# Two of the matmuls' operand buffers begin eight bytes later in on-chip memory

## The reference

```python
def first_block(x, ...):                       # two layers
    for layer in range(2):
        h = rmsnorm(x, attn_norm[layer])
        x = x + (even_mixer(h, ...) if layer == 0 else mla_mixer(h, ...))
        h = rmsnorm(x, ffn_norm[layer])
        x = x + (silu(h @ w_gate[layer]) * (h @ w_up[layer])) @ w_down[layer]   # 1024 -> 2816 -> 1024
    return rmsnorm(x, final_norm)

def second_block(x, ...):                      # one layer
    proj = rms_norm(x, g) @ w_in               # 1024 -> 3328
    y = rwkv7_mix(proj[:, :1792], ...)         # a recurrence over the tokens, in chunks
    o = diff_attention(...)
    h = x + rms_norm(concat(y, o) @ w_out, g)
    u = causal_dwconv(rms_norm(h, g) @ w_up)   # 1024 -> 5632
    return h + rms_norm((gelu(u[:, :2816]) * u[:, 2816:]) @ w_down, g)
```

## Time and profile before

| | us |
|---|---|
| median of 3 runs | 1925.72 |
| lowest, highest | 1923.92, 1926.21 |
| span of the profiled execution | 1924.0 |
| PE busy in it | 1890.1 |
| PEld busy | 1527.6 |
| DVE, ACT, POOL busy | 999.1, 740.1, 179.1 |

### The profile page before, as it was taken

How to read it: one execution, slowest core, us unless ns; L and a number is a source line. 1 busy time by engine, 2 the same in 40 slices (tenths; PEclk the granted TensorE clock), 3 DMA queues, 4 the chain that set the end, 5 groups by cost and what they waited for, 6 DMA issues and landing times.

```text
span 1924.0 us, 26779 instructions
## 1 busy us (share of the span) xinstructions
PE 1890.1 (98%) x10729; PEld 1527.6 (79%) x10729; DVE 999.1 (52%) x1418; ACT 740.1 (38%) x1111; POOL 179.1 (9%) x215
## 2 busy tenths in 40 slices
PE   9999999999999999999999999999999999999998
PEld 7875788888888777788888888777878778888887
DVE  5456453434325686553343434749563566656523
ACT  4247432222224575542222323554342454333322
POOL 1001210000001100010000000303551100000001
PEclk9999999999999999999999999999999999999999
DMA  6310133232322202123223232321120223232321
GB/s 201 105 44 1 50 99 98 87 109 87 105 92 80 72 23 66 45 91 105 91 87 109 88 109 87 100 88 44 24 67 25 88 77 109 87 108 89 107 90 66
DMA packets 137795, 158.74 MB, mean 83 GB/s; under 512 B 15976, under 2 KB 125552, under 8 KB 137712
## 3 DMA queue, kind: packets, MB, share of 16 engines
q1 hardware_dynamic: 136272, 155.01, 25.2%
q0 software_dynamic: 1440, 2.58, 0.5%
HBM read 153.89 MB, written 3.68 MB: 82 GB/s over the span
## 4 chain that ended last, share of the span: by engine, by line
PE 90%; DVE 6%; ACT 2%; issue 1%; DMA 0%; SPq 0%; POOL 0%; ACTq 0%; DVEq 0%
PE bank L2893 35%; PE bank L2926 16%; PE bank L2425 13%; PE bank L2450 3%; PE bank L2980 2%; PE bank L2569 2%; PE bank L2944 2%; PE bank L2839 1%; PE bank L2872 1%; PE bank L2597 1%; PE bank L2688 1%; PE bank L2584 1%; PE bank L2511 1%; PE bank L2541 1%; DVE XL L1589 1%
## 5 line engine op out<-in xcount | busy, mean ns | idle before, releaser
L2893 PE MATMUL bank<-XH,w_hi 128*128 128x512 f32 x992 | 386.8, 390 | 0.7 <-DVE arena L1889 0.7
L2893 PE MATMUL bank<-XL,w_hi 128*128 128x512 f32 x992 | 386.0, 389 | 0.0
L2893 PE MATMUL bank<-XH,w_lo 128*128 128x512 f32 x992 | 385.9, 389 | 0.0
L2893 PEld LDWEIGHTS bank<-XH,w_hi 128*128 128x128 f32 x992 | 186.2, 188 | 39.9 <-DVE arena L1889 0.9
L2893 PEld LDWEIGHTS bank<-XL,w_hi 128*128 128x128 f32 x992 | 186.2, 188 | 39.1 <-issue 0.5
L2893 PEld LDWEIGHTS bank<-XH,w_lo 128*128 128x128 f32 x992 | 186.2, 188 | 38.8
L2425 PE MATMUL bank<-XH,w_hi 128*128 128x512 f32 x448 | 178.7, 399 | 2.5 <-DVE w_lo L1582 2.4
L2425 PE MATMUL bank<-XH,w_lo 128*128 128x512 f32 x448 | 175.3, 391 | 0.0
L2425 PE MATMUL bank<-XL,w_hi 128*128 128x512 f32 x448 | 175.1, 391 | 0.0
L1582 DVE TENSOR_TENSOR w_lo<-w_raw,w_hi 128x2048 fp32r<-128x2048 f32 (+5 forms) x67 | 116.4, 1757 | 93.9 <-ACT w_hi L1036 93.5
L1936 DVE TENSOR_TENSOR w_lo<-w_raw,w_hi 128x2048 fp32r<-128x2048 f32 x24 | 55.0, 2292 | 174.2 <-ACT w_hi L1347 174.2
(11 more groups left out here) (459 smaller groups left out, 3336.1 us busy)
## 6 DMA issues: line engine op xcount, KB each, us to landing
w_raw<-in_ffn_w_gate SPq DMA_DIRECT2D x22, 1024.0 KB, 5.3
w_raw<-in_ffn_w_up SPq DMA_DIRECT2D x22, 1024.0 KB, 5.3
w_raw<-in_ffn_w_down SPq DMA_DIRECT2D x22, 1024.0 KB, 4.9
w_raw<-in_w_up SPq DMA_DIRECT2D x22, 1024.0 KB, 5.1
w_raw<-in_w_in SPq DMA_DIRECT2D x13, 1024.0 KB, 5.3
w_raw<-in_w_down SPq DMA_DIRECT2D x11, 1024.0 KB, 5.0
w_raw<-in_even_w_in SPq DMA_DIRECT2D x8, 1024.0 KB, 5.3
w_raw<-in_even_w_out SPq DMA_DIRECT2D x4, 1024.0 KB, 5.3
```

What stands on the lines that cost most here:

```text
L2893: m = pe.matmul(bank[b][:, :], w[:, k, P * c:P * (c + 1)], x[:, k, :], start=(k == 0 and j == 0), stop=(k == KT - 1 and j == 2))
```

## The change

The function that places a buffer takes an alignment; a buffer of two words is put ahead of `XH`, and `XH`, `XL` and the float32 view under them are placed at multiples of 8 bytes instead of 32. No instruction is added, removed or moved on any engine.

```diff
-        def sb(name, shape, dt=F32):
-            return ctx.enter_context(nc.sbuf_tensor(name, shape, dt))
+        def sb(name, shape, dt=F32, align=32):
+            return ctx.enter_context(nc.sbuf_tensor(name, shape, dt, align_bytes=align))
...
         X = sb("X", [P, KT, SEQ])
-        with nc.sbuf_tensor("under_split", [P, 2 * KT * SEQ], F32) as under_split:
+        sb("two_words", [P, 2])
+        with nc.sbuf_tensor("under_split", [P, 2 * KT * SEQ], F32, align_bytes=8) as under_split:
             pass
-        XH = sb("XH", [P, KT, SEQ], F32R)
-        XL = sb("XL", [P, KT, SEQ], F32R)
+        XH = sb("XH", [P, KT, SEQ], F32R, align=8)
+        XL = sb("XL", [P, KT, SEQ], F32R, align=8)
         w_raw = sb("w_raw", [P, 2, UW])
```

## The result

| | before | after |
|---|---|---|
| median, us | 1925.47 (4 runs) | 1963.79 (4 runs) |
| lowest to highest | 1923.92 to 1926.21 | 1961.72 to 1965.68 |
| span of the profiled execution | 1924.0 | 1962.7 |
| PE busy | 1890.1 | 1929.3 |

The kernel is slower by 38.3 us, a ratio of 1.02 with a 95% interval of 1.0188 to 1.0212. The prediction was 1968.7, range 1922 to 1985. TensorE is at the high level of its clock in both profiles (granted clock 0.995 and 0.997 of full speed).

What follows compares the result with a forecast made beforehand. PE was taken to bound the kernel, busy 1890.1 of 1924.0 us. Matmuls of 512 columns (40.4 us) and 256 columns (2.5 us) made +43 us, other parts 0: span 1967, median 1968.7 us, range 1922 to 1985.

Steps and rivals of the forecast that it cites:

- the 6120: Matmuls of 512 columns counted in L2893, L2425, L2926, L2980, L2839 and L2439; at 6.6 ns each, 40.4 us more.
- 24 is nearer to 32 than to 0: Reason for charging the new 24-byte operand distance the whole 6.6 ns a matmul seen at 32 bytes.
- Eight bytes as such: Operands beginning two words past a multiple of 16 bytes: taken as 0; no row showed a moving one.
- the second sign of being wrong: Forecast wrong altogether if the eight bytes matter in their own right on the moving side; no size given.
- A: Rival: nothing happens, under_arena's products are slow from its place far up in memory; 1925.7 us, chance 0.22.
- B: Rival: in L2893, L2425 and L2926 shifted reads lose half of the 12.9 ns on top; 1886 us, chance 0.12.
- C: Rival: 512 moving columns touch one more 16-byte line, 1.7 ns on each matmul; 1936 us, chance 0.08.
- D: Rival: the moving operand's start needs more reads, worse than 32 bytes, 13.2 ns each; +86 us, 2012 us, chance 0.08.

Runs made afterwards that it cites:

- the stretches: Not the model: matmuls alone, mostly 144 in L2893's three passes, operands' places varied; 227.0 ns a matmul at distance 0, 230.1 to 234.3 at thirty of 31 distances from 4 to 124 bytes.

## Why the prediction came out right

The direction, the mechanism (the rhythm of the matmul stream, through the operands' places) and the price of a matmul were right; some things in it were not.

**The sum.** L2893 is exact: 2976 x 6.6 ns = 19.6 us were forecast, and its three loops took 235.21 - 228.53 us twice and 224.31 - 217.94 once, 19.7 us. L2425 got 6.8 ns a matmul in a long piece (39.22 us for 168; 38.08 before) and about 6.4 on average of the pieces that can be compared, with 1344 of them 8.6 us, against 8.9 forecast. L2926 was over-sized: its pieces with activations moving went from 104.09 to 107.29 us, twice, and its 480 matmuls with weights moving lost 4.4 ns instead of 6.6, 2.1 us; 9.5 us were forecast and 8.5 came. L2450 had the wrong sign: 384 x 6.6 ns = +2.5 us were forecast, and it gained 2.0 ns each, -0.8 us. These two terms are 4.3 of the 4.9 us by which the forecast was too high. The step that failed in L2450 is the carrying of a price from 512 moving columns to 256; the stretches with 256 columns show that there most unequal distances are the faster ones. There is also a gap in the count: 240 matmuls of 512 columns on `XH`, `XL`, `w_hi` and `w_lo` in smaller groups (48 each in L2450, L2750, L3298 and L2872, 24 each in L2459 with L2462 and in L2489) are not among the 6120. At 6.6 ns they would have put 1.6 us more on the forecast; under 1 us came, 4 to 6 ns each in the pieces of L2750, L2459, L2489 and L3298 that can be compared.

**Why 24 bytes cost as much as 32.** The forecast took "24 is nearer to 32 than to 0". The choice was right and the reason wrong: the price doesn't grow with the distance. In the stretches 4 bytes already cost 5.3 ns, more than the 4.1 of 24 bytes with the moving operand in its old place. That the changed kernel's own pair costs the price of 32 bytes was luck: the prediction had no row for it.

**Eight bytes as such.** The prediction left the moving operand's eight bytes open and took them at nothing beside the distance. With both operands eight bytes off the model takes 232.1 ns at equal remainders, so they do count by themselves: the second sign of being wrong, that the eight bytes matter in their own right, came true beside the forecast. They add nothing at 32 bytes' distance, since the change and the 32 bytes alone both take 233.3 ns.

**The rest.** ACT, DVE and the transfers were put at 0, and nothing of them is seen in the time; L2944 was said to stay, and stayed (233.3 and 233.1 ns). A loses twice: the distance alone slows the model, and 224 bytes more heal `first_down`. The Trainium skill, "TensorE: Matmul & The Clock Gate", Part 2, gives TensorE two independent read ports, one for each operand. What the prediction drew from this for A, that the distance can't matter, doesn't hold here: it costs 37 us in the model with the weights 32 bytes further on. Whether the two ports are independent no run here shows. B (faster) came true only in L2450, for 0.8 us. C forecast 1.7 ns a matmul; with both operands eight bytes off it is 5.4, and with `XH` and `XL` at their old places and only the weights moved it is 6.6. The Trainium skill, "SBUF — State Buffer", specifications, says that each step to a new line of 16 bytes has a price; no run here shows such a price apart from the rhythm. D's 13.2 ns were not seen; the worst of all stretches, both operands 4 bytes off, is 10.8 above the fast one.

**What stays open** is why. The prediction laid it to the weight load that reads while the matmul streams. A load that is 81 ns shorter made a matmul 4.7 ns longer in line and 3.4 ns shorter at 32 bytes, where some 10 and 14 ns less were expected, and at 384 moving columns the distance makes no difference. So the length of the load isn't what is paid. An interplay of the two reads in time isn't excluded by that, nor shown. What is shown is a stream of float32r matmuls whose distance from start to start depends on the places of all its operands. The exception at 120 bytes is open too.

## What to carry to other kernels

When a matmul-bound kernel runs in float32r with 512 moving columns, look at the time from one matmul's start to the next: give all moving and stationary buffers the same remainder mod 256 and start them at multiples of 32 bytes, and look for the odd buffer that isn't (here `under_arena`, 1923.08 against 1925.35 us). A buffer added or resized between the activations and the weights cost 2% here without touching an instruction, while 32 bytes ahead of both cost nothing, so print the addresses when a time moves for no reason. Before carrying a price to another width of the moving operand, find a row with that width.

## What the hardware showed that wasn't expected

- One buffer is enough to lose the fast rhythm: `XL`, `w_hi` or `w_lo` alone off by 32 bytes costs 4.0, 4.9 or 6.2 ns a matmul in the mean of the whole stream.
- In the distances tried it comes back at 256 bytes, not at 128: at a distance of 128 bytes a matmul takes 232.4 ns, at 256 and 512 it takes 227.0.
- At 256 moving columns the in-line map is among the slower ones (119.8 against 116.7 ns in L2450 at -32 bytes), and at 384 there is no difference between 0 and 32 bytes (173.5 ns).
- bf16 matmuls of the same shape take 215.8 ns at distances of 0, 8 and 32 bytes, so the fast rhythm of float32r is still 11 ns longer than theirs.
